# A two-layer attention, hyena, Fourier and delta-rule block on one core: query norm and norm vectors folded into later operations, and some steps of the norms reordered

## The chip, the cores and the metric

The kernel runs on one core of one Trainium2 chip. The metric is the time of one execution in microseconds (us), from the device. The program names its engines PE (TensorE, matrix products), ACT (ScalarE), DVE (VectorE), POOL (GpSimd) and SP (SyncE, which here only issues loads).

## What is computed

Two layers over 256 latent and 256 context tokens of 1,024 features, in fp32. Cut to what this case touches:

```
h = rmsnorm(x, norm1) * (1 + sc1) + sh1
p = h @ w_in                                   # q, k, v, hyena, fnet, deltanet inputs
q, k = rmsnorm(q, gain[0]), rmsnorm(k, gain[1])    # over 64 features; latent tokens then get rope
s = softmax((q k^T) * 64**-0.5), two maps per head;  a = s0 - lam * s1
y_att = rmsnorm(a @ v, subln) * (1 - lambda_init)
y_dn  = rmsnorm(o, dn_norm) * silu(z)          # o: the gated delta rule, both directions
x = x + g1 * (sum_n sigmoid(h @ w_gate[n]) * (y_n @ w_branch[n])) @ w_o
x = x + g2 * relu(h2 @ w_mlp1)**2 @ w_mlp2,    h2 = rmsnorm(x, norm2) * (1 + sc2) + sh2
```

The last layer needs only the latent stream, so there most steps work on 256 tokens (two tiles of 128) instead of 512 (four tiles).

## The kernel before, in words

**Strips.** All weights pass through the core in strips of 512 x 256 (512 KB). SP loads a strip into one of four `raw` slots. ACT copies it, rounded to fp32r, into one of two `whl` slots (`split_hi`, L1201, two halves), and DVE or POOL writes the remainder beside it (`split_lo`, L1210). PE then multiplies a strip as three products of high and low parts (`mm3`, L537), for activations that are split alike (`hhl`). As there are two `whl` slots, `hi_ahead(n)` and `lo_ahead(n)` prepare the strip two places after strip n, once PE has finished strip n; PE meanwhile works on strip n+1. A late `split_lo` makes PE wait. Within deltanet, attention and hyena the remainders are POOL's; in the merge, the output projection (`wo`) and the MLP they are DVE's.

**Order of one layer.** `norm(li, 0)`, deltanet (`dn`, twelve blocks and a long chain of 128 x 128 products), then in `att` the strips dz, aq, ak, av (four each), twelve hyena strips, then `hyena`, `fnet`, `merge` (a loop over four branches), `wo`, `norm(li, 1)` and the MLP. Each engine runs its own program in a fixed order written by hand; semaphores (`S[...]`) join them.

**The attention's front.** ACT copies the query and key units from PSUM into `a_qk`. DVE squares and sums them (L2255) into 32 columns each of `small`; ACT makes the reciprocal roots (`stat_root`), of the queries half way through ak, of the keys half way through av. DVE then scales, gains and rotates the keys (`scale_and_turn`, L1275: times the root, L1276: times the gain, and for the latent tiles 2 and 3 four multiplications at L1285, a subtraction at L1287 and an addition at L1288) and signals `k_ready`. POOL does the same to the query tiles. It does `ahead` of dz, aq and ak, waits for the queries' root, and then puts one query tile behind each strip it prepares, starting with the first av strip. PE turns queries and keys (L921) after the first four hyena strips, `slots[0]`.

**The attention's units.** There are 16 units (tile, head) in layer 0 and 8 in layer 1. PE makes two score maps; DVE takes the row maximum (L2288) and scales it by -0.125 (L1902); ACT writes exp(0.125 s - m) with its row sum; DVE divides and combines the maps of the unit before (`combine`, L2276 and after), and then does the hyena convolutions of this unit's slot (`conv`, L1902 and L1907). The last unit's `combine` stands behind the last slot's convolutions. PE then turns the combined map (L639) and the convolved blocks (L995).

**After the attention.** ACT makes the root of the sub-norm; POOL multiplies each tile by the root (L2602) and by `subln` (L2603), PE turns it and ACT copies it out (`turned`, L1651). The same is done for deltanet by `token_norm` on DVE (root, silu(z), `dnnorm`; tiles 128 x 512), with its copy out.

**The norms over features.** For norm number n = 1, 2, 3 (n = 2 li + which) POOL squares and sums six of eight feature blocks and multiplies each block by the amplitude (L2469) as DVE finishes the residual of that block (L2412, `x_added`). ACT squares the last two blocks, PE sums over partitions, ACT takes the root (`rstd_ready`). DVE multiplies the even blocks by it (L2025) and POOL the odd ones (L2491, signal `hn_pool`); ACT writes the high part (`hhi_ready`), DVE the low part (`low`, L2018, signal `h_ready`). PE starts with block 0. Ahead of its last square ACT makes the high part of the second strip that PE needs after the norm, and DVE the low part.

**Queues.** SP's `load_vecs` (L1330) issues seven small loads per layer, five of them vectors broadcast to 128 partitions, for layer 1 after every engine has passed `enter`; the strip loads of the layer stand behind them.

## Time and profile before

| what | value |
|---|---|
| median of 3 runs | 2367.67 us (2367.27 to 2368.08) |
| the profiled execution, its own time | 2371.28 us |
| its span, first to last instruction | 2369.5 us |
| mean granted clock of PE | 0.971 |
| PE busy | 2190.6 us (92% of the span) |
| DVE busy | 1181.0 us (50%) |
| ACT busy | 860.0 us (36%) |
| POOL busy | 703.5 us (30%) |

The span is the time between the first and the last instruction that the profile holds; the execution's own time is 1.8 us longer, and 3.6 us over the median of the other runs. Busy time is an average over stages with different limits, so the table only says that PE is the engine to follow. Which engine holds PE up is read from the waits and from the timelines of single stretches.

### The profile page before, as it was taken

The numbers are of one execution on the slowest core, as the hardware profiler recorded it, in microseconds if no ns is written. First come the engines' busy times: TensorE is split into PE (matmuls) and PEld (weight loads), VectorE is DVE, ScalarE is ACT, GpSimd is POOL, SyncE is SP. The second block draws the span as 40 slices with busy tenths as digits, with TensorE's granted clock in tenths as the row PEclk, the third lists the DMA queues.
The fourth block names the chain that finished last, engine by engine and source line by source line (L and its number), as shares of the span: only waits on it lengthen the run. The fifth ranks groups of instructions, "written<-read, shape, count | busy, mean of one in ns | idle before, by whom it ended". The sixth has DMA issues, their size and how long they took to land.

```text
span 2369.5 us, 36486 instructions
## 1 busy us (share of the span) xinstructions
PE 2190.6 (92%) x13284; PEld 1840.1 (78%) x13284; DVE 1181.0 (50%) x1924; ACT 860.0 (36%) x1655; POOL 703.5 (30%) x626
## 2 busy tenths in 40 slices
PE   6998999998998999998999998988889788998998
PEld 3555778997665888876888886767789767998998
DVE  4644454436557233335433444454453664656664
ACT  2334323332452323233322322453324444545443
POOL 2532221247213111116210224333216642114220
PEclk8999999999999999999999999999999999999999
DMA  7412333332651122232233333210003322554554
GB/s 232 138 45 100 105 108 108 99 100 72 223 172 52 54 94 93 96 97 81 89 98 98 98 97 90 77 36 1 1 1 117 121 76 92 169 168 143 186 178 142
DMA packets 232531, 245.62 MB, mean 104 GB/s; under 512 B 10899, under 2 KB 229332, under 8 KB 231380
## 3 DMA queue, kind: packets, MB, share of 16 engines
q1 hardware_dynamic: 229344, 232.45, 31.1%
q10 hardware_dynamic: 3060, 11.49, 1.3%
q8 instruction: 78, 1.28, 0.2%
q14 instruction: 49, 0.40, 0.1%
HBM read 237.62 MB, written 6.29 MB: 103 GB/s over the span
## 4 chain that ended last, share of the span: by engine, by line
PE 75%; DVE 11%; POOL 5%; ACT 4%; issue 4%; DMA 2%; DVEq 0%; SPq 0%; ACTq 0%; POOLq 0%
PE psum L537 54%; PE psum L532 19%; DVE big L1898 5%; DVE big L1907 2%; POOL whl L1210 2%; PE psum L639 2%; ACT tmp L1403 1%; POOL big L2469 1%; ACT big L1403 1%; ACT whl L1201 1%; DMA raw<-in_w_ada_dram 1%; ACT big L1406 1%; POOL big L1285 1%; DVE big L1902 0%; DMA big<-in_hy_table_dram 0%
## 5 line engine op out<-in xcount | busy, mean ns | idle before, releaser
L537 PE MATMUL psum<-hhl,whl 128*128 128x512 f32 (+1 forms) x4416 | 836.4, 350 | 40.6 <-DVE hhl L2018 18.1
L537 PEld LDWEIGHTS psum<-hhl,whl 128*128 128x128 f32 x4416 | 709.7, 194 | 166.9 <-issue 47.1
L1201 ACT CAST whl<-raw 128x512 fp32r<-128x512 f32 x656 | 374.4, 618 | 942.1 <-PE psum L537 939.8
L1210 DVE TENSOR_TENSOR whl<-raw,whl 128x512 fp32r<-128x512 f32 x480 | 330.5, 730 | 487.0 <-ACT whl L1201 485.9
L532 PE MATMUL psum<-big 128*128 128x128 f32 (+5 forms) x2990 | 510.1, 334 | 50.1 <-DVE big L1898 24.9
L532 PEld LDWEIGHTS psum<-big 128*128 128x128 f32 (+2 forms) x2990 | 397.4, 198 | 135.5 <-issue 56.2
L537 PE MATMUL psum<-bigr,whl 128*128 128x512 f32 (+1 forms) x2688 | 471.2, 337 | 4.2 <-DVEq L2392 2.5
L537 PEld LDWEIGHTS psum<-bigr,whl 128*128 128x128 f32 x2688 | 415.7, 191 | 57.1 <-issue 4.7
L1210 POOL TENSOR_TENSOR whl<-raw,whl 128x512 fp32r<-128x512 f32 x176 | 232.3, 1342 | 401.1 <-ACT whl L1201 387.7
L1406 ACT COPY big<-psum 128x512 f32<-128x512 f32 (+1 forms) x340 | 190.7, 561 | 306.6 <-PE psum L532 201.3
L1898 DVE TENSOR_TENSOR big<-big,psum 128x512 f32<-128x512 f32 (+1 forms) x166 | 99.2, 597 | 149.6 <-PE psum L532 145.2
L537 PE MATMUL psum<-whl,hhl 128*128 128x256 f32 x1344 | 165.1, 285 | 5.7 <-POOL whl L1210 5.7
L537 PEld LDWEIGHTS psum<-whl,hhl 128*128 128x128 f32 x1344 | 163.3, 193 | 6.8 <-issue 3.4
L2569 POOL TENSOR_TENSOR big<-big,tmp 128x512 f32<-128x512 f32 (+1 forms) x64 | 64.6, 1022 | 349.2 <-DVE tmp L2389 348.3
L2545 POOL TENSOR_TENSOR big<-big,tab 128x512 f32<-128x512 f32 x48 | 61.1, 1274 | 296.0 <-ACT big L1406 222.4
L1262 POOL TENSOR_TENSOR tmp<-tmp 128x512 f32<-128x512 f32 (+1 forms) x32 | 28.7, 896 | 315.0 <-ACT tmp L1403 315.0
L639 PE MATMUL psum<-tab,big 128*128 128x128 f32 x528 | 85.6, 300 | 38.7 <-DVE big L1907 19.6
L639 PEld LDWEIGHTS psum<-tab,big 128*128 128x128 f32 x528 | 63.7, 152 | 64.6 <-issue 25.3
L1898 DVE TENSOR_TENSOR big<-big 128x512 f32<-128x512 f32 x80 | 69.0, 862 | 55.2 <-ACT big L1403 50.3
L1907 DVE SCALAR_TENSOR_TENSOR big<-psum,cols,big 128x510 f32<-128x510 f32 (+1 forms) x96 | 63.3, 660 | 3.4
L2469 POOL TENSOR_SCALAR big<-xT,amp 128x256 f32<-128x256 f32 x48 | 53.8, 1134 | 37.4 <-issue 27.1
L1902 DVE TENSOR_SCALAR big<-psum,cols 128x512 f32<-128x512 f32 (+1 forms) x48 | 31.8, 662 | 55.5 <-PE psum L537 37.2
(143 smaller groups left out, 1461.8 us busy)
## 6 DMA issues: line engine op xcount, KB each, us to landing
raw<-in_w_mlp_dram SPq DMA_DIRECT2D x128, 512.0 KB, 3.6
raw<-in_w_ada_dram SPq DMA_DIRECT2D x96, 512.0 KB, 4.6
raw<-in_w_in_dram SPq DMA_DIRECT2D x88, 512.0 KB, 3.6
raw<-in_w_gate_dram SPq DMA_DIRECT2D x64, 512.0 KB, 3.5
raw<-in_w_branch_dram SPq DMA_DIRECT2D x32, 512.0 KB, 3.5
raw<-in_w_o_dram SPq DMA_DIRECT2D x16, 512.0 KB, 3.5
hy_spectra<-big SPq DMA_DIRECT2D x2, 2560.0 KB, 8.6
big<-hy_spectra ACTq DMA_DIRECT2D x2, 1280.0 KB, 5.5
```

The costliest lines, as they stand in the source:

```text
L532: return nc.tensor.matmul(o_, a, b, start=start, stop=stop)
L537: m = nc.tensor.matmul(o_, a(p_), b(q_), start=first and i == 0, stop=last and i == 2, skip_group_check=shared)
L639: m = nc.tensor.transpose(bank[:, i * P:(i + 1) * P], s, ids)
L1201: nc.scalar.copy(whl[:, r, 0, ks], raw_of(n)[:, ks]).then_inc(S["hi_ready"], 1)
L1210: ins = eng.tensor_tensor(whl[:, r, 1, ks], raw_of(n)[:, ks], whl[:, r, 0, ks].bitcast(F32), ALU.subtract)
L1403: return nc.scalar.activation(o_, i_, fn, **kw)
L1406: return nc.scalar.copy(o_, i_)
L1898: step(V.tensor_tensor(o_, a, b, op), s_)
L1907: step(V.scalar_tensor_tensor(o_, a, sc, b, op0, op1), s_)
L2469: ins = G.tensor_scalar(hn[:, k, sl], xT[:, k, sl], amp[:, li, which, k, s_:s_ + 1], None, ALU.mult)
L2545: step(G.tensor_tensor(hd(s_["dI"]), hd(s_["A"]), over_heads(const(f"off{32 << lv}")), ALU.mult), SD["aoff_ready"][d])
L2569: G.tensor_tensor(m_acc[:, i, tk], m_acc[:, i, tk], tmp[:, i % 2, tk], ALU.add)\
```

## The change

It does six things.

1. Queries are no longer multiplied by their reciprocal root. The scores therefore stay unscaled by it, and the root (times 0.125) becomes the per-partition scale of the exponential, and of the maximum that goes into its bias.
2. The gains of queries and keys are multiplied once into four small rotary tables per side (`turns`, 128 x 64 each, eight small DVE operations), so tiles 2 and 3 have no gain step. POOL's query tiles wait only for the queries' sums (`stat_ready`) and start two strips earlier, behind the third ak strip.
3. `subln` and `dnnorm` are loaded as one column (one value per partition) and applied as the scale of the copy out, on ACT; the two multiplications by them on POOL and DVE go.
4. In norms 1 to 3 ACT squares the last blocks before it makes the high part of the strip, which moves behind the squares.
5. In norms 1 to 3 block 1 is scaled by DVE, and POOL waits for that before blocks 3, 5 and 7; the low part of block 0 comes right behind.
6. The last attention unit is combined ahead of the last convolutions.

```diff
-                step(eng.tensor_tensor(v, v, small[:, c0:c0 + 8].unsqueeze(2).to_broadcast([P, 8, 64]), ALU.mult))
-                step(eng.tensor_tensor(v, v, qkgain[:, 64 * which:64 * which + 64].unsqueeze(1)
-                                       .to_broadcast([P, 8, 64]), ALU.mult))
-                if m_ >= 2:
+                if which:
+                    step(eng.tensor_tensor(v, v, small[:, c0:c0 + 8].unsqueeze(2).to_broadcast([P, 8, 64]), ALU.mult))
+                if m_ < 2:
+                    step(eng.tensor_tensor(v, v, qkgain[:, 64 * which:64 * which + 64].unsqueeze(1)
+                                           .to_broadcast([P, 8, 64]), ALU.mult))
+                else:
...
-                    for dst, a, b in ((q4[0], xa, cs), (q4[1], xb, sn), (q4[2], xb, cs), (q4[3], xa, sn)):
+                    for dst, a, b in ((q4[0], xa, ca), (q4[1], xb, sb), (q4[2], xb, cb), (q4[3], xa, sa)):
...
@@ SP, load_vecs @@
+                for dst, src in ((subln, attn_subln[li]), (dnnorm, dn_norm[li])):
+                    sp.dma_start(dst, src.unsqueeze(1)).then_inc(vecs_loaded, 16)
...
@@ ACT, norm @@
                 f(tmp[:, 0, tk], xT[:, KD - 1, tk], ACT.Square).then_inc(S["last_sq"], 1)
+                if which:
+                    hi_ahead(act, first_strip["wo", li] + 7)
+                elif li:
+                    s0, u0, m0 = strip_loop(("mlp2", 1), li - 1)
+                    split_hi(act, s0 + 3 + RING, 3, 4, m0 + 8 + 3 * 8)
...
@@ ACT, turned and exp @@
+                    step(f(dst, hd(b), ACT.Identity, scale=gain) if gain is not None else copy(dst, hd(b)),
...
-                        step(f(a_P[:, h % 2, cc, 0:nk * P], b[:, 0:nk * P], ACT.Exp, scale=0.125,
+                        step(f(a_P[:, h % 2, cc, 0:nk * P], b[:, 0:nk * P], ACT.Exp, scale=q_scale(m_, h, cc),
                                bias=small[:, MAXC + 8 + par:MAXC + 9 + par],
...
@@ ACT, wo @@
-                for i in range(8):
+                for i in range(7):
...
@@ DVE, norm @@
+                scaled(0)
+                if nn:
+                    scaled(1)
+                    low(0)
+                    scaled(2)
+                    low(1)
...
@@ DVE, token_norm @@
-                    tt(v, v, over_heads(gain), MUL, S["o_normed"])
...
@@ DVE, att @@
+                for which in range(2):
+                    gain = qkgain[:, 64 * which:64 * which + 64].rearrange("p (a h f) -> p a h f", a=2, h=2)
+                    for i in range(4):
+                        half = gain[:, :, i % 3 > 0, :].unsqueeze(1).to_broadcast([P, 2, 2, 16])
+                        tt(turns[:, which, i], ropes[i % 2], half, MUL)
...
+                dve.wait_ge(S["stat_root"], 4 * li + 2)
+                ts(sm(QK_STAT, 32), sm(QK_STAT, 32), 0.125, None, MUL)
...
+                    if u == len(units) - 1:
+                        combine(u)
                     convs(slots[1 + u])
-                combine(len(units) - 1)
...
@@ POOL, norm @@
+                if n:
+                    nm, count = hn_ready(n, 1)
+                    pool.wait_ge(S[nm], count)
+                for k in range(3 if n else 1, KD, 2):
...
@@ POOL, attention @@
-                for key in ("dz", "aq", "ak"):
+                for key in ("dz", "aq"):
                     ahead(key, li)
-                pool.wait_ge(S["stat_root"], 4 * li + 2)
...
+                lo_ahead(pool, rest.pop(0))
+                lo_ahead(pool, rest.pop(0))
+                pool.wait_ge(S["stat_ready"], 3 * li + 2)
                 for m_ in tiles(li):
                     lo_ahead(pool, rest.pop(0))
                     scale_and_turn(pool, step, 0, [m_], a_P[:, 0], S["q_ready"])
...
-                    step(G.tensor_tensor(v, v, over_heads(subln), ALU.mult), S["o_normed"])
```

## Rows read from the trace of the kernel before

**Rows 1.** The chain of work that ended last, whole kernel: shares by engine (the page's fourth part).

```profile
PE 75%; DVE 11%; POOL 5%; ACT 4%; issue 4%; DMA 2%; DVEq 0%; SPq 0%; ACTq 0%; POOLq 0%
```

**Rows 2.** Waits: engine, line, what was waited for; us in total, times, longest us.

```profile
PE psum L537 <- POOL whl L1210: 20.6, 11, 4.7
```

**Rows 3.** Timeline of PE, layer 0, aq to first hyena strips: start us, us, what, [idle before].

```profile
507.39 46.32 PE L537 MATMUL psum<-whl,hhl 128*128 128x256 f32 x384
...
553.54 5.63 PE L537 MATMUL psum<-hhl,whl 128*128 128x512 f32 x24
...
563.90 7.36 PE L537 MATMUL psum<-hhl,whl 128*128 128x512 f32 x24 [4.73 <-POOL whl L1210]
...
574.44 10.03 PE L537 MATMUL psum<-hhl,whl 128*128 128x512 f32 x36 [3.18 <-POOL whl L1210]
```

**Rows 4.** Timeline of POOL in the same stretch.

```profile
537.29 3.02 POOL L1210 TENSOR_TENSOR whl<-raw,whl 128x512 fp32r<-128x512 f32 x2 [3.28 <-ACT whl L1201]
...
541.39 1.29 POOL L1276 TENSOR_TENSOR big<-big,vecs 128x512 f32<-128x512 f32 x1
...
555.32 3.73 POOL L1285 TENSOR_TENSOR big<-big,tab 128x256 f32<-128x256 f32 x4
...
559.87 0.91 POOL L1288 TENSOR_TENSOR big<-big 128x256 f32<-128x256 f32 x1
```

**Rows 5.** Stretch after one of these stalls: us, busy (x) by engine, PEclk, DMA share, GB/s.

```profile
563.90:567.90 4.00, 4.00 (x11) 3.13 (x12) 3.96 (x5) 0.00 (x0) 3.84 (x4) 0.57 0.44 135
```

**Rows 6.** Timeline of PE, layer 1, dz to first hyena strips.

```profile
1795.77 3.10 PE L537 MATMUL psum<-whl,hhl 128*128 128x256 f32 x24 [1.63 <-POOL whl L1210]
...
1802.84 40.55 PE L537 MATMUL psum<-whl,hhl 128*128 128x256 f32 x336
...
1845.95 7.50 PE L537 MATMUL psum<-whl,hhl 128*128 128x256 f32 x48 [2.57 <-POOL whl L1210]
...
1857.69 7.51 PE L537 MATMUL psum<-hhl,whl 128*128 128x256 f32 x48 [4.24 <-POOL whl L1210]
```

**Rows 7.** Timeline of POOL, layer 1, splits and a turned query tile.

```profile
1821.17 2.54 POOL L1210 TENSOR_TENSOR whl<-raw,whl 128x512 fp32r<-128x512 f32 x2 [3.23 <-ACT whl L1201]
...
1838.20 2.83 POOL L1285 TENSOR_TENSOR big<-big,tab 128x256 f32<-128x256 f32 x4
...
1841.81 0.74 POOL L1288 TENSOR_TENSOR big<-big 128x256 f32<-128x256 f32 x1
```

**Rows 8.** Timeline of DVE, layer 0, last key tile; last convolution and combination.

```profile
569.57 0.96 DVE L1288 TENSOR_TENSOR big<-big 128x256 f32<-128x256 f32 x1
...
700.83 1.53 DVE L1907 SCALAR_TENSOR_TENSOR big<-psum,cols,big 128x510 f32<-128x510 f32 x2
...
703.42 0.75 DVE L1907 SCALAR_TENSOR_TENSOR big<-big,small 128x512 f32<-128x512 f32 x1
```

**Rows 9.** Timeline of PE: ends of both attentions, and first matmuls after two norms.

```profile
704.23 1.12 PE L639 MATMUL psum<-tab,big 128*128 128x128 f32 x4 [3.09 <-DVE big L1907]
...
1119.84 5.35 PE L537 MATMUL psum<-hhl,whl 128*128 128x512 f32 x14 [6.82 <-DVE hhl L2018]
...
1481.03 8.65 PE L537 MATMUL psum<-hhl,whl 128*128 128x256 f32 x48 [6.88 <-DVE hhl L2018]
...
1935.63 1.11 PE L639 MATMUL psum<-tab,big 128*128 128x128 f32 x4 [4.45 <-DVE big L1907]
```

**Rows 10.** Timeline of ACT, layer 0, before the second norm.

```profile
1109.31 1.14 ACT L1201 CAST whl<-raw 128x512 fp32r<-128x512 f32 x2 [4.30 <-PE psum L537]
...
1110.89 0.61 ACT L1403 ACTIVATE tmp<-xT 128x512 f32<-128x512 f32 x1
```

**Rows 11.** Groups by line and form: x count | busy us, mean ns | idle before.

```profile
L2603 POOL TENSOR_TENSOR big<-big,vecs 128x512 f32<-128x512 f32 x6 | 8.0, 1327 | 0.5
...
L1403 ACT ACTIVATE big<-psum,small 128x512 f32<-128x512 f32 x32 | 22.0, 689 | 25.1 <-DVE small L1902 24.0 <-ACT big L1406 0.5 <-ACT big L1403 0.5
...
L1403 ACT ACTIVATE tmp<-psum 128x512 f32<-128x512 f32 x32 | 19.0, 594 | 1.9
```

More of the change, by code:

```diff
@@ L151, in build @@
         qkgain = vecs[:, 0:128]
-        subln = vecs[:, 128:256]
-        dnnorm = vecs[:, 256:384]
+        subln = vecs[:, 128:129]
+        dnnorm = vecs[:, 256:257]
         lamv = vecs[:, 384:640]
@@ L285, in reads_to, with hn_ready @@
             return sum(reads_out(n // 4, n % 4) for n in range(q + 1))
+        def hn_ready(n, k):
+            on_dve = k % 2 == 0 or (n and k == 1)
+            if on_dve:
+                return "hn_dve", (0 if n == 0 else 4 + 5 * (n - 1)) + (k // 2 + 1 if n == 0 or k == 0 else
+                                                                       2 if k == 1 else k // 2 + 2)
+            return "hn_pool", (0 if n == 0 else 4 + 3 * (n - 1)) + (k // 2 + 1 if n == 0 else k // 2)
         def dn_toks(li, blk):
@@ L1331, in load_vecs @@
                 enter(sp, ph(li, 0))
-                for dst, src in ((qkgain, attn_qk_gain[li].rearrange("a b -> (a b)")), (subln, attn_subln[li]),
-                                 (dnnorm, dn_norm[li]), (lamv, attn_lambda[li].rearrange("a b -> (a b)")),
+                for dst, src in ((subln, attn_subln[li]), (dnnorm, dn_norm[li])):
+                    sp.dma_start(dst, src.unsqueeze(1)).then_inc(vecs_loaded, 16)
+                for dst, src in ((qkgain, attn_qk_gain[li].rearrange("a b -> (a b)")), (lamv, attn_lambda[li].rearrange("a b -> (a b)")),
                                  (alog, dn_a_log[li].rearrange("a b -> (a b)")),
@@ L1649, in stat_root, with turned @@
                 rsqrt(v, v, n, S["stat_root"])
-            def turned(li, nm, br):
+            def turned(li, nm, br, gain=None):
                 for m_ in tiles(li):
                     b = filled_bank(act, (nm, li, m_))
-                    step(copy(y[:, br, :, m_ * P:(m_ + 1) * P], hd(b)), S["y_turned"])
+                    dst = y[:, br, :, m_ * P:(m_ + 1) * P]
+                    step(f(dst, hd(b), ACT.Identity, scale=gain) if gain is not None else copy(dst, hd(b)),
+                         S["y_turned"])
                     give_fill(act, (nm, li, m_))
@@ L1780, in hyena @@
                     anti_copy(li, 0, 1)
-                turned(li, "ya", ATT)
+                turned(li, "ya", ATT, subln)
                 act.wait_ge(filled, fill_at["ya", li, NT - 1] + 1)
@@ L1858, in mlp @@
                     last = li == DEPTH - 1 and hf == 1
-                    with act.Fori(0, 3 if last else 4) as i:
+                    with act.Fori(0, 3 if hf else 4) as i:
                         for kc in range(4):
                             split_hi(act, s0 + kc + RING, i, 4, m0 + 2 * kc + 2 + i * 8)
+                    for kc in range(3) if hf and not last else ():
+                        split_hi(act, s0 + kc + RING, 3, 4, m0 + 2 * kc + 2 + 3 * 8)
                     if last:
@@ L2010, in norm, with low, scaled @@
                 ss = range(2) if which == 0 else streams(li)
-                def low(k):
-                    if k % 2:
-                        dve.wait_ge(S["hn_pool"], KD // 2 * nn + k // 2 + 1)
-                    dve.wait_ge(S["hhi_ready"], KD * nn + k + 1)
-                    for s_ in ss:
-                        sl = slice(s_ * L, (s_ + 1) * L)
-                        ins = V.scalar_tensor_tensor(hhl[:, 1, k, sl], hn[:, k, sl],
-                                                     mod[:, li, 24 * which + k, s_:s_ + 1],
-                                                     hhl[:, 0, k, sl].bitcast(F32), ADD, SUB)
-                    signals(dve, ins, S["h_ready"])
-                for k in range(0, KD, 2):
+                def low(*ks):
+                    for k in ks:
+                        nm, count = hn_ready(nn, k)
+                        dve.wait_ge(S[nm], count)
+                        dve.wait_ge(S["hhi_ready"], KD * nn + k + 1)
+                        for s_ in ss:
+                            sl = slice(s_ * L, (s_ + 1) * L)
+                            ins = V.scalar_tensor_tensor(hhl[:, 1, k, sl], hn[:, k, sl],
+                                                         mod[:, li, 24 * which + k, s_:s_ + 1],
+                                                         hhl[:, 0, k, sl].bitcast(F32), ADD, SUB)
+                        signals(dve, ins, S["h_ready"])
+                def scaled(k):
                     if nn:
@@ L2222, in dn, with token_norm @@
                     amps(1, 1)
-                token_norm(li, 0, o_dn, dnnorm, DN, DS[1]["A"])
-            def token_norm(li, i, o_, gain, br, scratch):
+                token_norm(li, 0, o_dn, DS[1]["A"])
+            def token_norm(li, i, o_, scratch):
                 for m_ in tiles(li):
@@ L2489, in norm @@
                 pool.wait_ge(S["rstd_ready"], n + 1)
-                for k in range(1, KD, 2):
+                if n:
+                    nm, count = hn_ready(n, 1)
+                    pool.wait_ge(S[nm], count)
+                for k in range(3 if n else 1, KD, 2):
                     G.tensor_tensor(hn[:, k, tk], hn[:, k, tk], rstd[:, tk], ALU.mult).then_inc(S["hn_pool"], 1)
```

43 lines of the change are left out of this document (24 added, 19 removed).

## Prediction, made before the changed kernel ran

> **What bounds the kernel now.** I read the chain of waits first. It lies on PE for three quarters [rows 1], so an operation saved on POOL, DVE or ACT is worth only what PE waits for it. Then the list of waits: PE waits for POOL's strip remainders 20.6 us [rows 2]. Then the timelines where those waits lie. In layer 0 PE runs the ak and av strips without a gap, 384 matmuls in 46.32 us, thus 5.79 us a strip, to 553.7 us. Two hyena strips later it waits 4.73 and 3.18 us for POOL, and the matmuls after each wait take 7.36 us instead of 5.63 and 10.03 instead of 8.45 (36 at 5.63/24) [rows 3]. The cause is the clock: in the 4 us after the first wait the granted clock averages 0.57, so mostly the 1.2 GHz level [rows 5]. A wait of 3 us thus costs 1.7 us more. Loss in layer 0: 7.91 + 1.73 + 1.58 = 11.2 us. In layer 1 it is 2.57 and 4.24 us, with 7.50 and 7.51 us for strips that otherwise take 5.79: 10.2 us. But a wait of 1.63 us there left the next 24 matmuls at 3.10 us, nearly full speed [rows 6].
>
> The reason is on POOL: behind each of two splits stands a query tile of nearly 9 us, root and gain included, against 5.79 us per strip.
>
> **Queries on POOL, layer 0.** What is removed: the root of four tiles and the gain of two. The gain took 1.29 us [rows 4], the root about as long. The rotation of a tile takes 4.35 us where DVE is quiet (1838.20 to 1842.55) [rows 7] and 5.46 us where DVE works on the keys (555.32 to 560.78) [rows 4]. What is moved: all tiles start two strips earlier, past two splits each. Tiles 0 and 1 (1.3 us each) now sit behind the ak splits, where POOL has more than 3 us idle per strip [rows 4, 7]. Then I walk on. The first av split ends at 537.29 + 3.02 = 540.3; tile 2 to 544.7; the next split, 2.54 us [rows 7], to 547.3, and PE needs it at 553.7 - 5.8 = 547.9: in time. Tile 3 now meets the keys on DVE: 547.3 + 5.5 = 552.8, and the split behind it, again about 3.0, ends at 556. PE needs it at 553.6: a wait of 2.4 us, plus 1.7 us of low clock. Loss 4.1 instead of 11.2: **gain 7.1**. Bounds: 11.2 if the wait goes; 4 if POOL is later by a further 1 to 3 us.
>
> **Layer 1.** Tiles 2 and 3 alone. Split 1821.17 + 2.54 = 1823.7 [rows 7]; tile 2 to 1828.1; a split beside the keys' sums, 3.0, to 1831.1, needed at 1843.4 - 2 x 5.79 = 1831.8 [rows 6]; tile 3 to 1836.1; split to 1838.7, needed at 1837.6. A wait of 1.1 us, below the 1.63 that left the clock alone. The hyena strips of this layer are half as long and POOL barely keeps up, for which I take off 0.4: **gain 10.2 - 1.1 - 0.4 = 8.7**. Bounds 5 (wait over 2 us with low clock) and 10.
>
> The cover of both gains is that the keys be ready when PE turns them. DVE ended them at 570.5 [rows 8]; it loses two gain steps and the rivalry with POOL, so some 6 us earlier, against PE's new arrival about 581. The added wait of POOL (`stat_ready`) is for sums that are done ten microseconds ahead.
>
> **Last combination first.** DVE's last convolution ends at 702.36, the combination at 704.17 [rows 8], and PE had waited 3.09 us for it [rows 9]. In the new order PE turns the map under the convolution, which now ends at 704.1 in place of 702.4. PE's turn of block 11 came at 706.8, behind 2.6 us of other turns: now 704.2. **Gain 2.7**. Queued behind the moved combination are the convolutions and the blocks' turns, hence not the whole 3.1. Layer 1, 4.45 us of waiting, two convolutions behind it: **1.5**.
>
> **Norms.** ACT's last square came at 1110.89, behind a 1.14 us cast and the other square [rows 10]; it can run at 1110.2. PE then needs its three sums back to back, so 0.9 of it counts. The cast now stands behind the square and its wait for `x_added`; the DVE remainder behind the cast ends 1.2 us later, about 0.8 ahead of the root. At the end of layer 0 `dve_left` and with it SP's vector loads and the strip loads behind them are 1.2 us late; the strips they fetch are wanted over 10 us later. DVE takes block 1 first, then block 0's low part meets less of POOL: 0.5. PE's waits were 6.82 and 6.88 us [rows 9]. Norm 1: **1.4**; norm 2, where DVE's whole series decides: **0.9**; norm 3: 0, as the sums of POOL come last there. Blocks 3, 5 and 7 stand behind POOL's new wait and ACT and DVE wait for them, but PE needs them later. Bounds 0 and 4 together.
>
> **Norm vectors.** `subln` on POOL is 8.0 us in six steps [rows 11], but PE works on fnet strips meanwhile; only DVE's rivalry with POOL at the spectrum counts. Between nothing and 2, I take **0.8**. `dnnorm` on DVE in layer 1 runs beside the split that left PE waiting 1.63 us [rows 6]: **0.6**, between 0 and 1.5; in layer 0 PE has strips to work on, 0. The eight table products per layer (about 0.2 us each, estimated from a 0.91 us step of four times the columns) lie where DVE waits for tokens; the load of two columns in place of two broadcasts is the same count on SP's queue, and is waited for only after the norm. Both nothing; without that cover at most 2 us a layer. The new scale of the copies and of the 48 exponentials: an exponential with a bias column takes 689 ns, a plain copy activation 594 [rows 11], so a second column is bounded by 0 and another 95 ns. Sixty such steps make at most 5.7 us; ACT has gaps after nearly all of them, so I take 0.
>
> The Trainium skill speaks against this part: its page "ScalarE: Activation LUTs" says that every pointer operand of an ACTIVATE lengthens it by about 93 ns, and the 95 ns of rows 11 agree for the first. By that rule, all of it on the path, the gain would be 5.6 us smaller, an estimate.
>
> **Sum.** 7.1 + 8.7 + 2.7 + 1.5 + 1.4 + 0.9 + 0.8 + 0.6 = 23.7 us. Against the profiled execution's own 2371.3 that gives 2347.6; the median of the runs is 3.6 lower, so 2367.7 - 23.7 = **2344.0 us**.
>
> **Rivals.**
> - *POOL stays behind.* Query tiles cost more in the company of DVE's sums, both layers still stall over 2 us and PE falls to the low clock each time; the norms give nothing. For it: in layer 1 my margin at 1831.1 is 0.7 us. Against: two tiles' worth of root and gain are gone. Gain 4 + 5 + 2.7 + 1.5 = 13: **2355**. Chance 0.2.
> - *No wait at all.* Tile 3 is quick enough, or DVE's keys start later. Then 11.2 + 9.8 + 8 = 29: **2339**. Chance 0.15.
> - *The gain is given back.* PE comes earlier to the attention units and waits there for strips or for DVE instead. Against: loads are released by PE's own progress and move with it, and those units depend on nothing absolute. Gain under 4.7: **2365**. Chance 0.04.
> - *Slower: the exponential's scale.* Reading a column at ACT's scale makes each exponential long. It decides at the units: in each of 24, two exponentials stand between the maximum and the next combination. DVE's order leaves ACT about 1 us of room there. To pass no change, ACT must add 1 us of room plus 23.7/24 per unit, thus 1 us per exponential, more than its own 0.69. At 1.3 us more each, 2.6 - 1.0 = 1.6 a unit, 24 x 1.6 - 23.7 = 15 slower: **2382**. For it: no row shows a scale column. Against: the bias column costs 95 ns. Chance 0.03.
> - *It does not do what it says*: DVE's wait for the keys' root still holds `k_ready`, and PE waits at the turns (L921) in place of the strips. It would need the keys 10 us later than before. Chance 0.01, about 2367.
>
> My forecast has 0.57. The range, **2336 to 2356**, takes in the first two rivals and the bounds of the ACT columns. A measurement of this kernel tells 0.2% (4.7 us) from no change: faster 0.92, within 0.2% 0.05, slower 0.03.
>
> **What would show it.** Timeline of POOL: query tiles behind the third ak strip, without root, 4.4 to 5.5 us each for tiles 2 and 3. PE, layer 0: one wait near 553.6 of about 2.4 us, none of 4; layer 1: one near 1837 less the gains so far. First matmul of L921 about 7 us earlier relative to the strips. PE's wait for L1210 on POOL falls from 20.6 to below 8. The turn of the last map starts ahead of DVE's last convolution. ACT: both squares ahead of the cast. Wrong would be: waits of L921 for DVE's keys, a low clock after several waits, or exponentials above 0.8 us with DVE waiting for them.

## The result, and the profile after

The changed kernel takes 2350.12 us, the median of four runs (2349.53 to 2355.06), against 2367.88 for the kernel before in the same comparison: ratio 0.9929, 95% interval 0.9912 to 0.9946, so 17.8 us faster. I had forecast 2344.0, 23.7 us faster, in a range of 2336 to 2356. The profiled execution took 2350.20 us, with a span of 2348.4.

The whole times carry several us of chance, so I read the gain from stretches of TensorE's timeline. Each begins and ends at an instruction that both kernels have (the merge's table load is ScalarE's). "Front" is the stretch up to the first attention scores, "units" the loop of scores, exponentials and combinations behind it. Lengths in us; the forecast of 1.4 is for two rows together:

| stretch | before | changed | gain | changed, again | forecast |
|---|---|---|---|---|---|
| start to the first delta-net product | 82.48 | 79.89 | 2.6 | 86.79 | |
| delta net, layer 0 | 377.09 | 375.72 | 1.4 | 376.04 | 0 |
| front, layer 0: first dz product to first scores | 136.16 | 129.68 | 6.5 | 129.68 | 7.1 |
| units, layer 0: to the end of the last convolution block's turn | 112.06 | 112.52 | -0.5 | 112.26 | 2.7 |
| then to the merge's table load | 95.57 | 93.81 | 1.8 | 94.02 | 0.8 |
| then to norm 1's first sum | 307.67 | 306.64 | 1.0 | 306.62 | 1.4, with the next |
| norm 1: first sum to first product | 8.81 | 7.48 | 1.3 | 7.49 | see above |
| MLP, layer 0 | 352.32 | 353.34 | -1.0 | 353.36 | 0 |
| norm 2 | 8.87 | 8.19 | 0.7 | 8.19 | 0.9 |
| delta net, layer 1 | 293.64 | 290.15 | 3.5 | 290.25 | 0 |
| front, layer 1 | 104.05 | 96.49 | 7.6 | 96.49 | 9.3 |
| units, layer 1 | 58.88 | 60.49 | -1.6 | 60.46 | 1.5 |
| then to the merge's table load | 52.85 | 55.68 | -2.8 | 55.68 | 0 |
| then to norm 3's first sum | 180.60 | 178.79 | 1.8 | 178.80 | 0 |
| norm 3 | 4.01 | 4.19 | -0.2 | 4.19 | 0 |
| MLP, layer 1 | 188.77 | 189.67 | -0.9 | 189.70 | 0 |

The column "changed, again" is another execution of the same kernel, described below. All stretches but the start repeat within 0.35 us, and the start moved by 6.9. So I compare spans without the start. Before it is 2287.0 us (2369.5 - 82.48), after 2268.5: 18.5 us. The kernel before has one profile only, so how well its stretches repeat is not shown.

Chain of work that ended last, changed kernel; the line that answers to [rows 1]:

```profile
PE 71%; DVE 11%; issue 9%; ACT 4%; POOL 4%; DMA 1%; DVEq 0%; SPq 0%; ACTq 0%; POOLq 0%
```

Waits of PE in the changed kernel; this answers to [rows 2], 20.6 us before, where I had looked for less than 8:

```profile
PE psum L545 <- POOL whl L1218: 10.9, 9, 3.3
```

Timeline of PE, layer 0, ak strips to first scores, changed kernel (start us, us, what, idle before), for [rows 3]:

```profile
503.42 46.31 PE L545 MATMUL psum<-whl,hhl 128*128 128x256 f32 x384
...
553.07 20.95 PE L545 MATMUL psum<-hhl,whl 128*128 128x512 f32 x84 [3.34 <-POOL whl L1218]
```

Timeline of POOL in that stretch, for [rows 4]: tile 2's four products, then tile 3's products, difference and sum, then the splits.

```profile
536.62 2.83 POOL L1300 TENSOR_TENSOR big<-big 128x256 f32<-128x256 f32 x4
...
543.54 4.65 POOL L1300 TENSOR_TENSOR big<-big 128x256 f32<-128x256 f32 x4
548.27 1.07 POOL L1302 TENSOR_TENSOR big<-big 128x256 f32<-128x256 f32 x1
549.30 0.91 POOL L1303 TENSOR_TENSOR big<-big 128x256 f32<-128x256 f32 x1
550.29 5.58 POOL L1218 TENSOR_TENSOR whl<-raw,whl 128x512 fp32r<-128x512 f32 x4
```

There is one wait instead of two, as forecast, but 3.34 us long instead of 2.4. Tile 3 took 6.7 us beside VectorE's keys where I had put 5.5, and tile 2, alone, 4.3.

Timeline of PE, layer 1, for [rows 6]:

```profile
1821.80 11.74 PE L545 MATMUL psum<-whl,hhl 128*128 128x256 f32 x96 [1.81 <-POOL whl L1218]
...
1837.26 6.02 PE L545 MATMUL psum<-hhl,whl 128*128 128x256 f32 x48 [0.83 <-POOL whl L1218]
1843.79 1.70 PE L545 MATMUL psum<-hhl,whl 128*128 128x256 f32 x12 [0.51 <-POOL whl L1218]
...
1853.91 1.67 PE L540 MATMUL psum<-big 64*128 64x512 f32 x4 [2.03 <-ACT big L1422]
```

I had forecast one wait of 1.1 us here; there are three, 3.15 us together. The 96 matmuls behind the 1.81 us wait run at full speed (two strips in 11.74 us). Four first scores then take 1.67 us, where they take 1.13 at full clock.

Groups of ACT and DVE by form, changed kernel (busy us, mean ns, idle before): an exponential of [rows 11], now with a scale column, and the product that makes its bias.

```profile
L1419 ACT ACTIVATE big<-psum,small 128x512 f32<-128x512 f32 x32 | 24.9, 778 | 26.1 <-DVE small L1930 24.9 <-ACT big L1422 0.5 <-ACT big L1419 0.5
```

```profile
L1930 DVE TENSOR_SCALAR small<-small 128x1 f32<-128x1 f32 x48 | 10.3, 215 | 1.7
```

The second column costs ScalarE 89 ns (689 to 778). The Trainium skill's page "ScalarE: Activation LUTs" says under "What ACT_TABLE_LOAD costs" that each pointer operand of an ACTIVATE adds about 93 ns; the trace agrees.

### The profile page after: what moved, and what is told of

Same layout as the page of the kernel before. It is cut to its first block, busy times and chain, and to the rows that moved or that the text cites. A ratio compares the mean times of both kernels' runs of the same rounds, so it can differ in the third digit from the quotient of the medians.

```text
span 2348.4 us, 36476 instructions
## 1 busy us (share of the span) xinstructions
PE 2185.1 (93%) x13284; PEld 1834.1 (78%) x13284; DVE 1170.8 (50%) x1935; ACT 865.0 (37%) x1655; POOL 670.9 (29%) x607
## 4 chain that ended last, share of the span: by engine, by line
PE 71%; DVE 11%; issue 9%; ACT 4%; POOL 4%; DMA 1%; DVEq 0%; SPq 0%; ACTq 0%; POOLq 0%
PE psum L545 49%; PE psum L540 19%; DVE big L1924 5%; DVE big L1933 2%; PE psum L647 2%; POOL whl L1218 1%; ACT tmp L1419 1%; ACT big L1419 1%; POOL big L2610 1%; ACT whl L1209 1%; DMA raw<-in_w_ada_dram 1%; ACT big L1422 1%; DVE big L1928 1%; POOL big L2507 1%; DVE small L2325 1%
## 5 line engine op out<-in xcount | busy, mean ns | idle before, releaser
L1422 ACT COPY big<-psum 128x512 f32<-128x512 f32 (+1 forms) x328 | 183.3, 559 | 302.2 <-PE psum L540 202.1
L540 PE MATMUL psum<-raw,csil 128*32 128x256 f32 x768 | 56.4, 409 | 3.6 <-DMA raw<-in_w_ada_dram 3.5
```

The lines of the kernel that those rows point to most:

```text
L540: return nc.tensor.matmul(o_, a, b, start=start, stop=stop)
L1422: return nc.scalar.copy(o_, i_)
```

## The experiments

Each is the changed kernel with one edit. Every kernel ran beside the kernel before, whose medians were 2367.8 to 2368.9 us. "Without the start" is the profiled span less its first stretch; the changed kernel has 2268.5.

**1. The exponential's scale a constant.**

```diff
-ACT.Exp, scale=q_scale(m_, h, cc),
+ACT.Exp, scale=0.125,
-   q_scale(m_, h, cc), -1.0, MUL, MUL, s_=S["max_ready"])
+   -0.125, None, MUL, s_=S["max_ready"])
```

> The changed kernel with the exponential's scale a constant 0.125 again, and the product that makes its bias a product by the constant -0.125; the query's root is left out of the scores, all else stays. Theory A (the prediction's: the column costs nothing on the path, taken 0 of 0 to 5.7 us): within 1 us of the changed kernel, 2350. Theory B (the longer forms lie on the chain of a unit: 778 against 689 ns for an exponential, 214 against 154 ns for the bias, twice a unit, 24 units of which 16 in layer 0): up to 24 x 2 x 0.15 = 7.2 us faster, 2343; by the stages 112.5 to 107.7 us for the units of layer 0 and 60.5 to 58.1 in layer 1. In between if only ScalarE's or only VectorE's part counts. The exponentials should go back to 689 ns.

2353.4 us (2346.9 to 2354.5), 2268.2 without the start. From the last scores' start to the last turn's end the stretch fell from 12.40 to 11.59 us in layer 0 and from 12.46 to 11.35 in layer 1. From the first scores to the last, over all other units, it was 99.73 against 100.12 and 48.46 against 48.03. I call the first of these stretches the tail. The columns thus cost 1.9 us in this kernel, all in the last unit of each layer, where VectorE and ScalarE end last. In the other 22 units TensorE has strips to work on. Theory A holds for those and theory B for the two ends. This kernel leaves the query's root out of the scores, so it computes something else, while its instructions differ in that operand alone. The exponentials took 688 ns and the bias 154:

```profile
L1928 DVE TENSOR_SCALAR small<-small 128x1 f32<-128x1 f32 x50 | 7.7, 154 | 1.7
```

Little of the 1.9 us is the length that the columns add. Where the combination comes late, the tails are 13.10 and 11.86 us without columns (the kernel before) and 13.21 and 11.98 with them (run 2 below): 0.1 us each. The rest appears only with the combination ahead. In layer 0 TensorE waits 2.13 us for the last map here and 2.38 in the changed kernel, and the turns behind it run at a granted clock of 1.00 here and 0.50 there (four in 0.66 us against 1.11). So 0.25 us of the 0.8 is waiting, the rest the clock. In layer 1 VectorE comes to the combination 0.13 us sooner behind the last scores (5.15 us against 5.28). Its product by a column starts just ahead of GpSimd's split and keeps its 0.49 us; in the changed kernel it starts just behind the split and takes 1.47 (see run 2). DVE and then POOL in layer 1 of this run:

```profile
1912.64 0.49 DVE L1928 TENSOR_SCALAR big<-big,small 128x512 f32<-128x512 f32 x1
1913.17 1.63 DVE L1933 SCALAR_TENSOR_TENSOR big<-big,small 128x512 f32<-128x512 f32 x1
```

```profile
1912.69 3.23 POOL L1218 TENSOR_TENSOR whl<-raw,whl 128x512 fp32r<-128x512 f32 x2 [2.50 <-ACT whl L1209]
```

**2. The last combination behind the convolutions.**

```diff
-    if u == len(units) - 1:
-        combine(u)
     convs(slots[1 + u])
+combine(len(units) - 1)
```

> The changed kernel with the last combination behind VectorE's last convolution again, in both layers. Theory A (the prediction's): the path loses what I gave to the move, 2.7 us in layer 0 and 1.5 in layer 1, so 2354; the unit stages 112.5 to 115.2 and 60.5 to 62.0. Theory B (the last turns wait for the convolutions as much as for the combination, and the two only change places): within 0.7 us of the changed kernel in each layer. The observed stages of the changed kernel (no gain in either layer) fit B, or A with the column's cost laid over it: e1 beside this run tells which.

2351.0 us (2345.0 to 2354.4), 2270.1 without the start. The tail, last scores to last turn, is 13.21 us in layer 0 (12.40 in the changed kernel) and 11.98 in layer 1 (12.46). So the move was worth 0.8 us in layer 0 and cost 0.5 in layer 1, and theory A falls. That layer 0's whole unit stretch grew to 115.7 is not the move: its body before the last unit took 102.46 us against 100.12, with a wait of 2.18 us of TensorE for a load of `w_ada`. Behind the last unit, up to the merge, this run took 92.62 and 53.00 us, 1.2 and 2.7 less than the changed kernel, at a mean granted clock of 0.99 and 0.98 against 0.97 and 0.93; whether the move sets that is not shown (see below). The timelines show why so little is left. DVE in layer 0 with the combination late:

```profile
698.84 0.49 DVE L1928 TENSOR_SCALAR big<-big,small 128x512 f32<-128x512 f32 x1
699.37 0.75 DVE L1933 SCALAR_TENSOR_TENSOR big<-big,small 128x512 f32<-128x512 f32 x1
```

DVE and then POOL in layer 0 of the changed kernel, combination ahead:

```profile
691.00 0.90 DVE L1924 TENSOR_TENSOR small<-small 128x1 f32<-128x1 f32 x1
691.93 1.46 DVE L1928 TENSOR_SCALAR big<-big,small 128x512 f32<-128x512 f32 x1
693.43 0.75 DVE L1933 SCALAR_TENSOR_TENSOR big<-big,small 128x512 f32<-128x512 f32 x1
```

```profile
690.61 2.50 POOL L1218 TENSOR_TENSOR whl<-raw,whl 128x512 fp32r<-128x512 f32 x2 [13.71 <-ACT whl L1209]
```

Ahead of the convolutions the combination meets GpSimd's split. Its small product takes 0.90 us instead of 0.16 and the next 1.46 instead of 0.49: 1.7 us lost. The convolutions between, which read PSUM, take 1.53 us in either place, and in this run they lie beside the split. DVE and POOL, layer 0, combination late:

```profile
696.77 1.53 DVE L1933 SCALAR_TENSOR_TENSOR big<-psum,cols,big 128x510 f32<-128x510 f32 x2
```

```profile
695.72 2.50 POOL L1218 TENSOR_TENSOR whl<-raw,whl 128x512 fp32r<-128x512 f32 x2 [13.69 <-ACT whl L1209]
```

The Trainium skill, page "SBUF — State Buffer", "Who interferes with whom", says that VectorE's instructions with two SBUF inputs or in a two-port mode hold a port pair that GpSimd also needs, and that one with at most one SBUF input, outside those modes, does not contend; these rows fit it. In layer 1 both wide steps are hit, and two convolutions still follow, whose blocks TensorE now waits for. DVE, changed kernel, then POOL, then PE:

```profile
1907.22 1.47 DVE L1928 TENSOR_SCALAR big<-big,small 128x512 f32<-128x512 f32 x1
1908.73 1.64 DVE L1933 SCALAR_TENSOR_TENSOR big<-big,small 128x512 f32<-128x512 f32 x1
```

```profile
1907.14 2.67 POOL L1218 TENSOR_TENSOR whl<-raw,whl 128x512 fp32r<-128x512 f32 x2 [2.45 <-ACT whl L1209]
```

```profile
1910.42 1.12 PE L647 MATMUL psum<-tab,big 128*128 128x128 f32 x4 [2.92 <-DVE big L1933]
1911.98 0.69 PE L1003 MATMUL psum<-tab,big 128*128 128x128 f32 x2 [0.44 <-DVE big L1933]
1913.71 0.69 PE L1003 MATMUL psum<-tab,big 128*128 128x128 f32 x2 [1.05 <-DVE big L1933]
```

One wait of 4.45 us [rows 9] became three, of 4.41 together.

**3. The query's tiles one strip earlier, the rotated ones first.**

```diff
 lo_ahead(pool, rest.pop(0))
-lo_ahead(pool, rest.pop(0))
 pool.wait_ge(S["stat_ready"], 3 * li + 2)
-for m_ in tiles(li):
-    lo_ahead(pool, rest.pop(0))
-    scale_and_turn(pool, step, 0, [m_], a_P[:, 0], S["q_ready"])
+order = [2, 0, 3, 1] if li == 0 else [2, None, 3]
+for m_ in order:
+    if m_ is not None:
+        scale_and_turn(pool, step, 0, [m_], a_P[:, 0], S["q_ready"], order[-1])
+    lo_ahead(pool, rest.pop(0))
```

> The changed kernel with the query's tiles one strip earlier and the rotated ones ahead of the plain ones: behind the first ak strip tile 2, then 0, 3, 1 with one split between each in layer 0; tile 2 behind the first and tile 3 behind the third in layer 1. GpSimd then does tile 3 of layer 0 from about 524 to 529 us, ahead of VectorE's key sums (from 529) instead of beside its keys' turns (4.65 us for four products there, 2.83 alone). Theory A (TensorE's waits of 3.34 us in layer 0 and 1.81 + 0.83 + 0.51 in layer 1 are GpSimd's late splits, and nothing else is late behind them): 4 to 6 us faster than the changed kernel, 2345, and no wait of TensorE over 1 us on a split in either stretch. Theory B (VectorE's keys or the first convolutions end last there by then): the waits go and the first scores come at most 1 us earlier.

2342.4 us (2339.1 to 2346.0), ratio to the kernel before 0.9892 (0.9877 to 0.9908), faster than both kernels. Without the start it has 2260.5, 8.0 less than the changed kernel. The fronts are 124.47 and 94.30 us, 5.2 and 2.2 shorter: theory A. PE and POOL, layer 0:

```profile
551.94 19.23 PE L545 MATMUL psum<-hhl,whl 128*128 128x512 f32 x84
```

```profile
526.69 2.83 POOL L1301 TENSOR_TENSOR big<-big 128x256 f32<-128x256 f32 x4
```

No wait is left in layer 0 (layer 1 keeps two, of 0.68 and 0.49 us), and the same 84 matmuls take 19.23 us instead of 20.95. So of the 5.2 us, 3.34 were the wait and 1.7 the clock behind it. Tile 3's products take 2.83 us away from VectorE's keys, not 4.65.

**4. The tiles behind the av strips again, but short.**

```diff
-lo_ahead(pool, rest.pop(0))
-lo_ahead(pool, rest.pop(0))
-pool.wait_ge(S["stat_ready"], 3 * li + 2)
+for _ in range(4):
+    lo_ahead(pool, rest.pop(0))
+pool.wait_ge(S["stat_root"], 4 * li + 2)
```

> The changed kernel with the query's tiles behind the av strips and the wait for the query's root again, as before the change, with the shortened tiles. Theory A (shortening does half: a rotated tile is 2.6 us shorter, two of them stand ahead of a split that TensorE waits for, so the 11.2 us lost in layer 0 become about 6 and the 10.2 of layer 1 about 5): 4 to 5 us slower than the changed kernel, 2355, two thirds of the front's gain stays. Theory B (the earlier start does nearly all): 10 us slower than the changed kernel, 2360. Theory C (shortening does all): within 1 us of the changed kernel.

2353.0 us (2349.8 to 2355.7), 2268.9 without the start, within 0.4 us of the changed kernel. Layer 0's front is even 0.9 us shorter (128.83). Layer 1's is 2.0 longer (98.46): there TensorE waits 3.04 us, and the 48 matmuls behind take 7.40 us. But its first four scores then take 1.13 us instead of 1.67, and from the first to the last scores it has 46.48 us against 48.03. PE, layer 0:

```profile
557.00 5.74 PE L545 MATMUL psum<-hhl,whl 128*128 128x512 f32 x24 [1.63 <-POOL whl L1218]
...
564.89 8.46 PE L545 MATMUL psum<-hhl,whl 128*128 128x512 f32 x36 [2.15 <-POOL whl L1218]
```

In layer 0 two short waits, with the matmuls behind them near full speed, cost no more than one of 3.34 us with 1.7 us of low clock. The shorter tiles without the earlier start gave 7.3 and 5.6 us of the fronts' gain (136.16 to 128.83, 104.05 to 98.46). That is theory C in sum and A in layer 1's front: the earlier start as the change placed it gave nothing in sum.

**5. The bias by a negated column, one operation.**

```diff
+ts(sm(640, 32), sm(QK_STAT, 32), -0.125, None, MUL)
-   q_scale(m_, h, cc), -1.0, MUL, MUL, s_=S["max_ready"])
+   small[:, 640 + 8 * m_ + 2 * h + cc:641 + 8 * m_ + 2 * h + cc], None, MUL, s_=S["max_ready"])
```

> The changed kernel with a second set of 32 columns, the query's scale negated, so that a unit's bias is one product by a column instead of a product by a column and one by -1. It parts VectorE's share of the column's price from ScalarE's: e1 took both away, and from the last scores' start to the last turn's end the stretch fell from 12.40 to 11.59 us in layer 0 and from 12.46 to 11.35 in layer 1. Theory A (the second operation makes the form longer): the bias takes 154 ns again as with a constant, and the two tails fall by about 0.1 us each, so that ScalarE's exponentials hold the rest. Theory B (the pointer does): 214 ns stay, and nothing falls. The whole time can't tell them apart; the stretches and the mean of the form can.

2355.4 us (2351.3 to 2361.0), 2269.6 without the start. The form's mean is 212 ns (50 instructions, two of them the vectors' products), the tails 12.38 and 12.45. Theory B: the column makes it longer, not the second operation.

**6. The last square behind the casts again.**

```diff
-                if which:
-                    hi_ahead(act, first_strip["wo", li] + 7)
-                elif li:
...
-                for i in range(7):
+                for i in range(8):
```

> The changed kernel with the last square behind the casts again in norms 1 and 2 (two casts of ScalarE move back ahead of it), all else as changed. Theory A (the prediction's: the squares' turn was the whole of norm 1's 1.4 us and most of norm 2's 0.9): the wait from the norm's first sum to the first product that reads the normed input grows from 7.48 to 8.8 us in norm 1 and from 8.19 to about 8.9 in norm 2, 2 us in all. Theory B (block 1 on VectorE is what shortened it): both stay within 0.2 us of 7.48 and 8.19, and the next run shows the loss.

2354.8 us (2350.9 to 2357.1), 2270.6 without the start. Norm 1 is 8.05 us instead of 7.48, and the stretch ahead of it 307.69 instead of 306.62, since the first sum too waits for a square behind a cast: 1.6 us together, theory A there. Norm 2 stays at 8.11, so its gain is not the squares'. The edit reaches norm 3 too, which takes 5.08 us instead of 4.19; but so it does in runs 1, 2, 3, 8 and 11, which have no edit there, so nothing follows from it. ACT in the changed kernel, for [rows 10]: square, casts, then the root, which waits 0.19 us for the sum where it waited 1.55.

```profile
1098.44 0.63 ACT L1419 ACTIVATE tmp<-xT 128x512 f32<-128x512 f32 x1 [2.09 <-DVE xT L2450]
1098.97 1.12 ACT L1209 CAST whl<-raw 128x512 fp32r<-128x512 f32 x2
1100.28 0.69 ACT L1419 ACTIVATE rstd<-psum,tab 128x512 f32<-128x512 f32 x1 [0.19 <-PE psum L540]
```

**7. Block 1 on GpSimd again.**

```diff
-            on_dve = k % 2 == 0 or (n and k == 1)
...
+            return "hn_pool" if k % 2 else "hn_dve", KD // 2 * n + k // 2 + 1
```

> The changed kernel with block 1 of norms 1 to 3 scaled on GpSimd again. Theory A (the first product waits for block 0 alone, so block 1 sets only the second wait): the first waits stay at 7.48 and 8.19 us, and TensorE's second wait in norm 1 grows from 0.51 to between 1 and 2 us; total 1 to 2 us. Theory B (ordering of the squares did all): no difference in any norm.

2350.1 us (2348.6 to 2351.9), 2269.2 without the start. Norm 1 stays at 7.49, norm 2 grows from 8.19 to 8.94, which is its whole gain. Neither theory has it: A looked for a longer second wait behind norm 1, B for nothing. In fact that second wait, 0.51 us in the changed kernel, is gone here. The MLP behind norm 1 is 1.7 us shorter than in the changed kernel (351.67) and the delta net behind norm 2 is 1.1 longer (291.25). Run 3 has 351.29 for that MLP with block 1 on VectorE and the 0.51 us wait, so most of the 1.7 is not shown to be the edit's. PE's first product behind norm 2, this kernel and then the changed one:

```profile
1466.27 8.98 PE L541 MATMUL psum<-hhl,whl 128*128 128x256 f32 x48 [6.88 <-DVE hhl L2041]
```

```profile
1467.27 1.62 PE L545 MATMUL psum<-hhl,whl 128*128 128x256 f32 x6 [6.12 <-DVE hhl L2045]
```

**8. The two norm vectors as products over rows again.**

```diff
-turned(li, "ya", ATT, subln)
+turned(li, "ya", ATT)
+step(G.tensor_tensor(v, v, over_heads(subln), ALU.mult), S["o_normed"])
...
-turned(li, "yd", DN, dnnorm)
+turned(li, "yd", DN)
+tt(v, v, over_heads(dnnorm), MUL, S["o_normed"])
```

> The changed kernel with the sub-norm and delta-norm vectors as products over rows again (GpSimd's second product of each of the 4 and 2 tiles, VectorE's third), their copies out without a column. Theory A (the prediction's): 0.8 us for GpSimd's products in the stretch from the last unit to the merge's table load in layer 0, and 0.6 us at the end of layer 1's delta net; nothing in layer 1's own end and layer 0's delta net, where others end last. Theory B (the copies' column, 688 against 594 ns, eats it): no difference. The stretch from the last unit of layer 0 to the merge fell from 95.6 to between 92.6 and 94.7 us over the runs so far, 2 us more than part 3 was given, so it could also be worth more than 0.8.

2358.2 us (2356.0 to 2360.8), 2270.1 without the start. Layer 0's stretch from the last unit to the merge grew from 93.8 to 97.7 us, 3.9, five times what I gave the part. Layer 1's front grew by 0.4, the end of its delta net not at all. DVE and PE in this run:

```profile
714.55 1.52 DVE L1924 TENSOR_TENSOR big<-big 128x512 f32<-128x512 f32 x1
...
720.00 1.75 DVE L1924 TENSOR_TENSOR big<-big 128x512 f32<-128x512 f32 x1
```

```profile
717.50 3.78 PE L540 MATMUL psum<-big 128*128 128x512 f32 x4 [2.69 <-DVEq L1190]
720.30 7.48 PE L545 MATMUL psum<-hhl,whl 128*128 128x512 f32 x24
```

The product of spectrum and signal at 714.55 reads SBUF alone and takes 1.52 us beside GpSimd's eight sub-norm products (709.36 to 719.54), 0.68 alone; the one at 720.00 lies beside GpSimd's next step. VectorE's chain there ends last, TensorE's wait is 2.69 us instead of 1.64, and the 24 matmuls behind it run at a low clock, 7.48 us instead of 6.05. The kernel before has the same wait (2.72 us) and the same slow matmuls (7.64), and yet its stretch is 95.6 us, 2.1 shorter than here, at a mean granted clock of 0.97 against 0.93. So the 3.9 us are not the worth of this part alone.

**9. The changed kernel again.** No edit.

> The changed kernel itself once more, to part what its executions do by chance from what the edits do. In the profiled executions so far three stretches took two lengths each without an edit in them: the start up to the first delta-net product 79.8 or 84.3 us, the one from layer 1's last unit to its merge 53.0 or 55.7, the delta net of layer 1 290.1 or 294.4, the last two with the same waits of TensorE and different granted clocks. Theory A (chance of the execution): at least one of the three comes out at its other length, and all stretches that hold an edit stay within 0.3 us of the first profile (fronts 129.68 and 96.49, norm stretches 7.48 and 8.19). Theory B (the kernel sets them, through where its gaps lie): all three repeat at 79.9, 55.7 and 290.15.

2354.4 us (2351.9 to 2357.5), 2268.9 without the start: theory B, but for the start, whose 86.79 us are neither of the lengths that theory A named. The stretches are the kernel's, down to their low clock.

**10. Early tiles, and layer 1's combination late.** The edits of 3 and of 2, the latter for `li == 1` alone.

> The early tiles of the third experiment, and the last combination behind the convolutions in layer 1 alone, where moving it ahead lengthened the stretch from the last scores to the last turn's end from 11.98 to 12.46 us; layer 0 keeps it ahead (13.21 to 12.3). If both hold by themselves: fronts 124.5 and 94.3 us, tails 12.3 and 12.0, and 0.5 us faster than the early tiles alone, too little for the whole time to show; against the changed kernel 7 to 8 us faster, 2342, with stretches whose length is chance left aside.

2345.2 us (2339.4 to 2347.7), 2261.8 without the start. Fronts 124.48 and 94.29, tails 12.29 and 11.97, each as expected. But layer 1's units took 49.6 us up to the last scores, against 48.8 in run 3, and the sum is 1.3 us worse than there. The early tiles alone remain the best version.

**11. The table products four times over.**

```diff
-for i in range(4):
+for i in (0, 1, 2, 3) * 4:
```

> The changed kernel with each of the eight products a layer that put the query's and key's norm vectors into the rotary tables made four times over, 24 small products a layer more on VectorE, 0.2 to 0.57 us each, so 5 to 14 us of VectorE a layer. Theory A (the prediction's cover: they lie in an idle stretch ahead of the query's squares, and GpSimd waits for these only one strip later): the front stretches stay within 0.3 us of 129.68 and 96.49. Theory B (VectorE's queue there is tight): the query's squares and so tile 2 come late, by up to 10 us in layer 1, where VectorE's products took 0.57 us each beside GpSimd.

2352.6 us (2346.7 to 2357.2), 2271.0 without the start. The fronts are 129.71 and 96.52 us: the cover holds. The 2.5 us over the changed kernel lie mainly in norm 3 (5.08 us) and the MLP behind it (190.8), far from the edit. In layer 1 the products took 14.7 us on VectorE, and the first scores did not move:

```profile
1781.20 14.71 DVE L1924 TENSOR_TENSOR big<-tab,vecs 128x64 f32<-128x64 f32 x32
```

## Why the prediction was right, and where it was off

**Queries on POOL, layer 0: 6.5 us for 7.1.** The mechanism held: one wait near 553, one stretch of low clock behind it. The mis-sized number is tile 3, which I let take 5.5 us in the keys' company; it took 6.7. Run 4 adds that the step "all tiles start two strips earlier" had no worth in layer 0 as placed: it put tile 3 beside the keys and joined two short waits to one behind which the clock was low. Run 3 shows what the start can give, 5.2 us more, which is my rival of no wait at all.

**Layer 1: 7.6 for 9.3** (8.7 and `dnnorm`'s 0.6). The waits were 1.81, 0.83 and 0.51 us for the 1.1 and 0.4 that I had put, and they left the clock alone, as I had it. `dnnorm` measured 0.4 in run 8, but not where I put it: the wait of 1.63 us [rows 6] is still 1.59 in the changed kernel and the same in run 8.

**Last combination first: 0.8 for 2.7, and -0.5 for 1.5.** This is the step that failed. I took the combination's duration from rows where it ran alone, and moved it to where GpSimd's split runs. The 1.7 us lost in layer 0 are most of what lies between 0.8 and 2.7; in layer 1, 3.11 us for the two wide steps against 1.23 is more than the 1.5 I gave the move.

**Scale columns: 0 taken, 1.9 measured in the two tails.** "ACT has gaps after nearly all of them" is true of 22 units, and the two exceptions were on the path. Two parts of it I did not count: VectorE's own column (154 to 215 ns), and that the last unit has no strips behind it. But this cost and the last one do not add up: with the combination late the columns cost 0.1 us a tail, and with constant scales the move ahead gains 1.5 us in layer 0 (13.10 to 11.59) and 0.5 in layer 1 (11.86 to 11.35). A shift of 0.1 to 0.3 us decides what the combination meets and whether the clock falls.

**The units as a whole: -2.1 for 4.2.** The two tails together gained 0.1 us (13.10 to 12.40, 11.86 to 12.46). The loss lies ahead of the last scores, where I had forecast nothing. In layer 0 that part grew by 1.2 us (98.97 to 100.12), at a granted clock of 1.00 in both kernels; TensorE's waits for loads of `w_ada` grew there from 2.9 to 3.5 us, and the part varies between 98.9 and 102.5 over the runs, so the 1.2 is put down to no edit. In layer 1 it grew by 1.0 (47.02 to 48.03), at a clock of 0.93 against 0.96; run 4, whose first scores run at full clock, has 46.48.

**Norms: total close, split wrong.** Norm 1 gave 2.4 with the stretch ahead of it, 1.4 forecast; run 6 confirms 1.6 of it for the squares. Norm 2 gave 0.7 for 0.9, but through block 1, and the new order also brought a second wait of 0.51 us behind norm 1. I put norm 3 at 0, and the stretch itself gave nothing. The one ahead of it became 1.8 us shorter, but it lies between 178.4 and 180.8 us in the runs, most of which have no edit there, so its cause stays open.

**Sub-norm: 0.8 taken, 1.8 seen, 3.9 between run 8 and the changed kernel.** I named the right mechanism, VectorE's rivalry at the spectrum, with a bound of 2: it moves TensorE's wait by 1.05 us. The rest is clock, and how much of that belongs to this part is open, as run 2 has 92.6 us there and the kernel before 95.6.

**What no step held: the clock takes part of it back.** In layer 1 the change saved the low clock in the front. It then stands at the first scores (four matmuls 1.67 us instead of 1.13; run 4, which has it in the front, has 1.13) and again behind the last unit, where there was little before. Window of the changed kernel and of run 3 behind the last unit and ahead of the merge (us, busy and count of PE, PEld, DVE, ACT, POOL, PEclk, DMA share, GB/s):

```profile
1914.40:1922.40 8.00, 7.68 (x37) 5.82 (x35) 0.21 (x1) 1.95 (x6) 0.00 (x0) 0.70 0.00 0
1954.40:1962.40 8.00, 8.00 (x37) 6.02 (x36) 2.73 (x5) 3.51 (x6) 0.00 (x0) 0.85 0.14 49
```

```profile
1911.90:1919.90 8.00, 6.71 (x36) 4.85 (x35) 1.15 (x2) 2.86 (x10) 0.00 (x0) 0.83 0.01 2
1951.90:1959.90 8.00, 8.00 (x46) 7.24 (x45) 2.73 (x5) 3.89 (x7) 0.00 (x0) 1.00 0.00 0
```

PE's 20 matmuls there, changed kernel and then run 3, behind the same wait:

```profile
1953.62 6.98 PE L540 MATMUL psum<-big 128*128 128x512 f32 x20 [2.66 <-DVE big L1924]
```

```profile
1950.12 5.44 PE L540 MATMUL psum<-big 128*128 128x512 f32 x20 [2.67 <-DVE big L1925]
```

The stretch is 55.6 to 55.9 us in the changed kernel, in its second execution and in runs 4 to 8 and 11. It is 52.9 before and 53.1, 53.0, 53.1 and 53.2 in runs 1, 2, 3 and 10. Its instructions are the same in all, and TensorE's idle time in it is 6.0 to 6.4 us in each. So 2.8 us of the gain went here. Which edit sets it is not clear: the runs with a tail of under 12 us ahead of it have the short length, those with 12.4 to 12.5 the long one, but run 3 has 12.46 and the short one. The opposite sign is in the delta net of layer 1, 3.5 us faster without an edit in it but for the order of blocks in norm 2. It stays so in the second execution, but run 3 has 294.4 and run 10 has 290.0, and these two differ only behind it. Run 3 has the pattern of the kernel before: 48 matmuls in 7.46 us behind a wait of 1.78 for GpSimd, and later 12 in 4.68, where the changed kernel has 5.98 behind 0.83 and 3.10. So the low clock falls in other places there. What decides between the two lengths is not settled, and none of the 3.5 us counts for the change's reasons.

The sum of the table: 14.0 us from the two fronts, -2.1 from the units, 1.8 at the spectrum of layer 0, 2.4 at norm 1 with the stretch ahead of it, 0.7 at norm 2, 1.6 at norm 3 and ahead of it, -2.8 to the clock behind layer 1's units, and 2.9 net in the four stretches without an edit that follow the start. That is 18.5 against a forecast of 23.7. Below the forecast are the units (6.3), the clock (2.8) and the two fronts (2.4); above it are the spectrum and norm 1 (1.0 each) and stretches that I had at nothing (1.6 and 2.9). The steps that I named gave 16.8 us. That the sum came to 18.5 is luck: 4.5 us that no run ties to the change, less the 2.8 of clock.

## What to carry to other kernels

A step moved to a new place does not keep its duration: look up what the neighbour engine does at the new place, above all for VectorE's steps on SBUF beside GpSimd's. Two edits on one path need not add up: 0.1 us of length cost 1.1 us where it changed which engine came first. Count a cost where each engine ends last, unit by unit; the last unit of a loop has no cover. A wait on TensorE costs its length plus what the clock takes behind it, so two short waits can be cheaper than one long, and a saving of some us should be read stretch by stretch, since the clock can take it back at the next gap.

## What was not expected of the hardware

- A 128x512 product by a column on VectorE that starts 0.05 us ahead of GpSimd's split keeps its 0.49 us; one that starts 0.08 us behind it takes 1.47.
- A column operand lengthens VectorE's 128x1 product from 154 to 212 ns; a second operation with a constant adds nothing (215).
- Beside a GpSimd split a 128x512 product by a column on VectorE takes 1.46 us instead of 0.49, and a 128x1 product 0.90 instead of 0.16, while steps that read PSUM keep their 1.53.
- Two executions of one program had all 15 later stretches equal within 0.35 us, low clock included, and differed by 6.9 us in the first 80.
